# A fused decoder layer on one core: the expert biases move from the thirteenth pair of experts to the tenth, and the last pair gets another assignment of PSUM banks and another order on TensorE

## The reference, cut to what matters here

```python
def moe_ffn(hx, ...):                       # hx: 288 x 1024
    logits = hx @ w_router + b_router       # 32 experts
    top_val, top_idx = lax.top_k(logits, 4)
    comb = ...                              # 288 x 32: softmax of the four, 0 elsewhere
    def expert_step(acc, xs):               # for each of the 32 experts
        gu = hx @ wgu + bgu                 # 1024 -> 2048
        gate = jnp.minimum(gu[:, 0::2], 7.0)
        up = jnp.clip(gu[:, 1::2], -7.0, 7.0)
        act = gate * jax.nn.sigmoid(1.702 * gate) * (up + 1.0)
        y = act @ wdn + bdn                 # 1024 -> 1024
        return acc + c[:, None] * y
hx = layer_norm(DN_ALPHA * hx + moe_ffn(hx, ...), ln2_g, ln2_b)
```

## Time and profile before

| | |
|---|---|
| median of 3 runs | 1140.02 us (1139.33 to 1140.36) |
| the profiled execution | 1139.37 us, span 1137.5 us |
| TensorE busy | 1099.5 us, 97% of the span |
| VectorE, ScalarE busy | 293.1 us (26%), 203.6 us (18%) |
| DMA | 454.37 MB, mean 399 GB/s, over 420 GB/s in most slices after the first quarter |
| chain that ended last | PE 83%, DMA 13%, ACT 2%, DVE 2% |

### The profile page before, as it was taken

How to read it: one execution, slowest core, us unless ns; L and a number is a source line. 1 busy time by engine, 2 the same in 40 slices (tenths; PEclk the granted TensorE clock), 3 DMA queues, 4 the chain that set the end, 5 groups by cost and what they waited for, 6 DMA issues and landing times.

```text
span 1137.5 us, 14116 instructions
## 1 busy us (share of the span) xinstructions
PE 1099.5 (97%) x5468; PEld 463.2 (41%) x5469; DVE 293.1 (26%) x734; ACT 203.6 (18%) x481; POOL 30.0 (3%) x65
## 2 busy tenths in 40 slices
PE   8999999999999999999999999999999999999996
PEld 6876764433333333333333333333333333333331
DVE  1553757530303030212121212120203031303033
ACT  2323412411111120202020202020201111111102
POOL 0110111000000000000000000000000000000001
PEclk9999999999999999999999999999999999999998
DMA  9967878999999999999999999999999999999994
GB/s 361 351 219 248 285 280 336 426 433 407 430 421 430 430 431 430 431 430 429 432 431 432 432 430 432 432 432 429 433 430 432 432 430 432 431 430 430 425 426 160
DMA packets 59172, 454.37 MB, mean 399 GB/s; under 512 B 6467, under 2 KB 19411, under 8 KB 31348
## 3 DMA queue, kind: packets, MB, share of 16 engines
q1 hardware_dynamic: 56642, 440.97, 92.7%
q0 software_dynamic: 1728, 10.75, 2.5%
q10 hardware_dynamic: 754, 1.98, 0.4%
HBM read 450.14 MB, written 11.93 MB: 406 GB/s over the span
## 4 chain that ended last, share of the span: by engine, by line
PE 83%; DMA 13%; ACT 2%; DVE 2%; issue 1%; SPq 0%; DVEq 0%
PE bank L1171 30%; PE bank L1224 19%; DMA ring<-in_w_gate_up 13%; PE bank L732 6%; PE bank L759 6%; PE bank L1055 5%; PE bank L1251 3%; PE bank L762 2%; PE bank L920 2%; PE bank L1051 1%; PE bank L1354 1%; PE bank L1267 1%; PE bank L877 1%; ACT ybuf L1417 1%; ACT actT L1417 1%; PE bank L851 1%
## 5 line engine op out<-in xcount | busy, mean ns | idle before, releaser
L1171 PE MATMUL bank<-ring,xg 128*64 128x512 f32 x2032 | 445.6, 594 | 10.8 <-DMA ring<-in_w_gate_up 10.8
L1171 PEld LDWEIGHTS bank<-ring,xg 128*64 128x64 f32 x2032 | 146.4, 137 | 299.3 <-issue 296.9
L1224 PE MATMUL bank<-ring,actT 128*64 128x512 f32 x960 | 216.2, 597 | 4.2 <-ACT actT L1417 4.2
L2080 DVE TENSOR_TENSOR acc<-acc,bank 128x512 f32<-128x512 f32 x60 | 41.3, 688 | 492.0 <-PE bank L1251 491.8
L1571 ACT ACTIVATE sig<-gate 128x256 f32<-128x256 f32 x64 | 26.5, 416 | 530.1 <-DVE gate L2062 530.1
L1224 PEld LDWEIGHTS bank<-ring,actT 128*64 128x64 f32 x960 | 67.3, 137 | 120.0 <-issue 115.3
L2062 DVE TENSOR_SCALAR gate<-bank 128x256 f32<-128x256 f32 x64 | 26.8, 419 | 186.8 <-PE bank L1171 186.8
L759 PE MATMUL bank<-xT,wblk 128*128 128x288 f32 x256 | 65.4, 409 | 0.3 <-DVE xT L1670 0.3
L1562 ACT ACTIVATE xg<-bank,small 128x128 f32<-128x128 f32 x128 | 48.0, 457 | 97.0 <-PE bank L732 96.9
L1055 PE MATMUL bank<-hx,pick 128*128 128x512 f32 x128 | 59.2, 605 | 0.0
L1417 ACT ACTIVATE ybuf<-bank 128x512 f32<-128x512 f32 x63 | 36.0, 596 | 126.7 <-PE bank L1224 87.4
(11 more groups left out here) (247 smaller groups left out, 672.3 us busy)
## 6 DMA issues: line engine op xcount, KB each, us to landing
ring<-in_w_gate_up SPq DMA_DIRECT2D x127, 2048.0 KB, 26.5
ring<-in_w_down SPq DMA_DIRECT2D x63, 2048.0 KB, 28.0
wblk<-in_w_in SPq DMA_DIRECT2D x11, 1024.0 KB, 8.7
kring<-in_cache_k_moba SPq DMA_DIRECT2D x16, 256.0 KB, 7.5
vring<-in_cache_v_moba SPq DMA_DIRECT2D x16, 256.0 KB, 7.2
out<-in_state_k_win POOLq DMA_DIRECT2D x8, 512.0 KB, 5.2
out<-in_state_v_win POOLq DMA_DIRECT2D x8, 512.0 KB, 6.1
kring<-in_state_k_win SPq DMA_DIRECT2D x16, 256.0 KB, 5.3
```

Source lines behind the costliest of these rows:

```text
L1171: ins = nc.tensor.matmul(bank[n][64 * e:64 * e + 64, :], xg[:, k, 64 * e:64 * e + 64], w[e][:, 512 * n:512 * n + 512], start=False, stop=( ...
L1224: ins = nc.tensor.matmul(bank[4 + half][64 * e:64 * e + 64, :], actT[:, j, 64 * e:64 * e + 64], w[e][:, at:at + 512], start=(j == 0), stop ...
L2080: V.tensor_tensor(o, o, new, ALU.add).then_inc(S.added, 1)
```

## The change

Two parts. `MIDDLE` becomes 9: the biases are added in pair 9, and pairs 9 to 15 instead of 12 to 15 are written out on TensorE. In the last pair, `combine` of pair 14 follows gate/up step k = 1 instead of k = 3; tile 0 and the samples are brought into banks 4, 5 and 7 after k = 4, ahead of gate/up's end; both halves of the activations are transposed into bank 6, the first behind a wait for the copy of the weights out of that bank; down's sums go to banks 0 and 1; the rest follows the new assignment of banks.

```diff
+    Y_BANK, SUM_BANK = (0, 1), ((4, 5), (2, 3), (7,))
...
-    MIDDLE = 12
+    MIDDLE = 9
...
         finish(MIDDLE + 1, MIDDLE // PERIOD, 1, MIDDLE // PERIOD)
+        finish(MIDDLE + 2, MIDDLE // PERIOD, 2, MIDDLE // PERIOD + 1)
+        finish(MIDDLE + 3, MIDDLE // PERIOD + 1, 0, MIDDLE // PERIOD + 1)
+        finish(MIDDLE + 4, MIDDLE // PERIOD + 1, 1, MIDDLE // PERIOD + 1)
         last = PAIRS - 1
...
-            return nc.tensor.matmul(bank[2 * t + half][:, :], ident, acc[:, t, 512 * half:512 * half + 512],
+            return nc.tensor.matmul(bank[SUM_BANK[t][half]][:, :], ident, acc[:, t, 512 * half:512 * half + 512],
                                     start=True, stop=stop)
 
-        def last_down():
-
-            turn_act(last, 2 * last + 2, (0,))
+        def keep_first():
             pe.wait_ge(S.added, 5 * last + 5)
             keep_sums(0, 0)
             keep_sums(0, 1)
-            pe.wait_ge(S.actT_ready, last * 2 + 1)
             keep_sums(2, 0)
+
+        def turn_last(a):
+            pe.wait_ge(S.act_ready, last * 4 + 2 * a + 2)
+            pe.wait_ge(*((S.actT_ready, 2 * last + 1) if a else (S.spread_ready, last + 1)))
+            for j in range(4 * a, 4 * a + 4):
+                f = 512 * a
+                ins = turn(bank[6][:, 128 * (j % 4):128 * (j % 4) + 128], up[:, f + j % 4:f + 512:4])
+            ins.then_inc(S.act_turned, 1)
+
+        def last_down():
+
+            turn_last(0)
             for v in range(4):
...
-                            ins = nc.tensor.matmul(bank[4 + half][64 * e:64 * e + 64, :], actT[:, j, 64 * e:64 * e + 64],
+                            ins = nc.tensor.matmul(bank[Y_BANK[half]][64 * e:64 * e + 64, :], actT[:, j, 64 * e:64 * e + 64],
...
                 if v == 0:
-                    turn_act(last, 2 * last + 2, (1,))
+                    turn_last(1)
                     keep_sums(1, 0)
...
-        gate_up(last, last // PERIOD, 0, {3: lambda: combine(last - 1), 5: lambda: turn_weights(last, 2 * last + 1)})
+        gate_up(last, last // PERIOD, 0, {1: lambda: combine(last - 1), 4: keep_first, 5: lambda: turn_weights(last, 2 * last + 1)})
         last_down()
         mix_last()
...
-        take_turned(PAIRS - 1, (0,))
+        take_turned(PAIRS - 1, (0,), (6, 6))
         sigmoids(PAIRS - 1, (2, 3))
-        take_turned(PAIRS - 1, (1,))
+        take_turned(PAIRS - 1, (1,), (6, 6))
```

More of the change, by code:

```diff
@@ L1329, in keep_sums @@
             if t == 2:
-                return nc.tensor.matmul(bank[7][:, 0:256], ident, acc_s[:, :], start=True, stop=stop)
-            return nc.tensor.matmul(bank[2 * t + half][:, :], ident, acc[:, t, 512 * half:512 * half + 512],
+                return nc.tensor.matmul(bank[SUM_BANK[2][0]][:, 0:256], ident, acc_s[:, :], start=True, stop=stop)
+            return nc.tensor.matmul(bank[SUM_BANK[t][half]][:, :], ident, acc[:, t, 512 * half:512 * half + 512],
                                     start=True, stop=stop)
-        def last_down():
-            turn_act(last, 2 * last + 2, (0,))
+        def keep_first():
             pe.wait_ge(S.added, 5 * last + 5)
@@ L1370, in mix_last @@
                 if t == 2:
-                    ins = mix_samples(bank[7], False)
+                    ins = mix_samples(bank[SUM_BANK[2][0]], False)
                 else:
-                    ins = nc.tensor.matmul(bank[j][:, :], spread[:, 128 * t:128 * t + 128],
+                    ins = nc.tensor.matmul(bank[SUM_BANK[t][half]][:, :], spread[:, 128 * t:128 * t + 128],
                                            ybuf[:, 512 * half:512 * half + 512], start=False, stop=True)
                 ins.then_inc(S.mixed, 1)
-        gate_up(last, last // PERIOD, 0, {3: lambda: combine(last - 1), 5: lambda: turn_weights(last, 2 * last + 1)})
+        gate_up(last, last // PERIOD, 0, {1: lambda: combine(last - 1), 4: keep_first, 5: lambda: turn_weights(last, 2 * last + 1)})
         last_down()
@@ L1575, in take_weights, with take_turned @@
             copy(spread[:, :], bank[6][:, 0:T]).then_inc(S.spread_ready, 1)
-        def take_turned(i, halves=(0, 1)):
+        def take_turned(i, halves=(0, 1), banks=(7, 6)):
             for a in halves:
                 act.wait_ge(S.act_turned, i * 2 + (a + 1))
-                copy(actT[:, 4 * a:4 * a + 4, :], bank[7 - a][:, :].rearrange("p (k s) -> p k s", k=4)).then_inc(
+                copy(actT[:, 4 * a:4 * a + 4, :], bank[banks[a]][:, :].rearrange("p (k s) -> p k s", k=4)).then_inc(
                     S.actT_ready, 1)
@@ L1636, in take_lower @@
             act.wait_ge(S.down_done, PAIRS)
-            copy(ybuf[:, 0:512], bank[4][:, :]).then_inc(S.y_ready, 1)
+            copy(ybuf[:, 0:512], bank[Y_BANK[0]][:, :]).then_inc(S.y_ready, 1)
         nc.scalar.activation(s_(c_junk), s_(c_junk), ACT.Sqrt)
@@ L1649, in _ @@
         for half in range(2):
-            nc.scalar.activation(acc[:, 0, 512 * half:512 * half + 512], bank[half][:, :], ACT.Identity,
+            nc.scalar.activation(acc[:, 0, 512 * half:512 * half + 512], bank[SUM_BANK[0][half]][:, :], ACT.Identity,
                                  bias=mv[:, 2:3], scale=mv[:, 1:2]).then_inc(S.y_centred, 1)
@@ L2138, in take_upper @@
             dve.wait_ge(S.down_done, PAIRS)
-            V.tensor_copy(ybuf[:, 512:1024], bank[5][:, :]).then_inc(S.y_ready, 1)
+            V.tensor_copy(ybuf[:, 512:1024], bank[Y_BANK[1]][:, :]).then_inc(S.y_ready, 1)
         def sums_to_sbuf():
@@ L2144, in sums_to_sbuf @@
                 t, half = divmod(j, 2)
-                o, new = (acc[:, t, 512 * half:512 * half + 512], bank[j][:, :]) if t < 2 else (acc_s[:, :], bank[7][:, 0:256])
+                o, new = (acc[:, t, 512 * half:512 * half + 512], bank[SUM_BANK[t][half]][:, :]) if t < 2 else (acc_s[:, :], bank[SUM_BANK[2][0]][:, 0:256])
                 dve.wait_ge(S.mixed, 5 * last + n + 1)
@@ L2159, in y_statistics @@
                 dve.wait_ge(S.mixed, 5 * last + after + half)
-                step.on(V.bn_stats(s_(c_stat + 12 * t + 6 * half, 6), bank[2 * t + half][:, :]))
+                step.on(V.bn_stats(s_(c_stat + 12 * t + 6 * half, 6), bank[SUM_BANK[t][half]][:, :]))
             dve.wait_ge(step.sem, step.n)
@@ L2196, in _ @@
             c = slice(512 * half, 512 * half + 512)
-            gain_and_bias(acc[:, 1, c], bank[2 + half][:, :], mv[1][:, 0:1], mv[1][:, 1:2], ln2_g_sb[:, c], ln2_b_sb[:, c])
+            gain_and_bias(acc[:, 1, c], bank[SUM_BANK[1][half]][:, :], mv[1][:, 0:1], mv[1][:, 1:2], ln2_g_sb[:, c], ln2_b_sb[:, c])
     ctx.close()
```

## The result

| | before | changed |
|---|---|---|
| median (lowest to highest), 11 runs each | 1141.07 us (1139.33 to 1142.12) | 1144.03 us (1142.09 to 1144.80) |
| profiled execution, span | 1139.37, 1137.5 us | 1142.41, 1140.6 us |
| ratio | | 1.0021, 95% interval 1.0014 to 1.0029 |

The changed kernel is slower by some 2.4 us (1.6 to 3.3 by the interval; the medians lie 2.96 apart). Forecast were 0.9 us more and "within 0.2%"; the ratio lies at that bound. The median of 1144.03 us lies outside the forecast range of 1139.3 to 1142.3. A part of that distance, 1.05 us, is no effect of the change: the 11 runs of the kernel before have a median of 1141.07, where the forecast added its 0.9 to the 1140.02 of the three runs shown.

The account below looks back on a forecast made before the run. The prediction took the DMA queue's weights, 58.35 us a pair, to set the pace mid-kernel. Its terms, 0 + 0 + 0.9 + 0, added to the median 1140.02 us, gave 1140.9 us, range 1139.3 to 1142.3.

Parts of the forecast that it names:

- The biases' place is worth nothing: Biases moved from pair 12 to 9: TensorE's 4.8 us is caught up waiting for weights either way; 0 us.
- The waits of about 1 us in pairs 12 to 14: Sign of being right: TensorE waits about 1 us for weights in gate/up of these pairs.
- The rival by which they would be worth 4.8 us: TensorE bounds from pair 12 to the end, so moving the biases wins 4.8 us: 1136.1 us; chance 0.08.
- The loops that become straight code cost nothing that the rows show: Newly written-out pairs on TensorE: 0 us, since pair 14, already straight, takes 55.95 us.
- its signs of being wrong: Pair 15's bias rows near 1062, weight wait in last pair, down's clock under 1.00, DVE awaiting a DMA before statistics.
- nothing to lose, since the wait that remains is the queue's: Bound on the biases' move, at pair 14's step 6: at most 0.14 us to gain, no loss.
- The last pair: Gate/up's end to down: moved identity products and uncovered activation copy cost net +0.9 us, between +0.75 and +1.0.
- The identity products after k = 4: Tile 0 and the samples, moved into the last pair's gate/up, add 2.3 us there (2.15 to 2.35).
- the way from transposes to down: Last pair: transposes, then ACT's copy with nothing between, put down's start 1.53 us after the transposes start.
- the cover that is lost: Last pair: identity products no longer run during ACT's copy; the old 2.91 us to down is subtracted.
- LayerNorm rows: Last LayerNorm's gain and bias, issued 2.3 us later: cost 0, 1.1 us cover; rival, DVE waits, 1142.2 us, chance 0.05.
- clock: Rival: TensorE's clock falls in the joined gap before the last pair's down, +3.6 us, 1144.5 us; chance 0.04.

Follow-up runs that it names:

- the second time: The unmodified changed kernel run once more against the kernel before: median 1144.22 against 1141.80 us, ratio 1.0025 (1.0013 to 1.0036).

## Why the prediction was wrong

*The biases' place is worth nothing: right.* The waits of about 1 us in pairs 12 to 14 are there (1.72 at 922.94, 0.95 at 981.18 and 1039.52), TensorE runs at the pace of the weights in both kernels, and the biases in pair 2 bring nothing either. The rival by which they would be worth 4.8 us had read the chain alone.

*"The loops that become straight code cost nothing that the rows show": wrong,* and this is the step that failed. I had tested it on TensorE's own time for a written-out pair (55.95 us), where it costs nothing indeed. But I had just found that the DMA engines and not TensorE set the pace, and did not ask what the code does to those. The page of the kernel before lists 34 packets of instructions in queue q8, and the windows show none of them in the looped stretch up to 892 us and two in each written-out pair. The runs show what six more of them do: about 1.0 us in the mean of the traces (1.6 against 0.6 above), 1.4 in the profiled execution. The bias rows of pair 15 start at 1069.11, not at the 1067.1 that the forecast named; among its signs of being wrong it had only an earlier start. I also gave the term the wrong bound: "nothing to lose, since the wait that remains is the queue's" takes the queue's pace for fixed.

*The last pair: right in kind, undersized.* Forecast 0.9, measured 1.18. The identity products after k = 4 cost 1094.38 - 1092.04 = 2.34 (2.3 forecast), the way from transposes to down 1.52 (1.53). Two terms were off: I took the 2.91 of the chain for the cover that is lost, where the time line's own 2.84 answers to it, 0.07; and gate/up now runs in four blocks instead of three, of 7.01, 10.46, 3.59 and 7.09 us where it was 13.89, 7.02 and 7.09, so 0.15 more. By the end of down both are on the path.

*LayerNorm rows and clock: cost 0, as forecast.* DVE starts its statistics 1.2 us behind the start of TensorE's first product, as before, without a wait for the DMA issued at 1111.11. The forecast had the cover shrink from 2.5 to 1.1 us; it grew to 3.6, since the last issue moved by 2.1 us and not with gate/up's end, while DVE's start moved by 3.15. The granted clock in down is 1.00, and its steps keep 3.65 us.

**Together:** 1.2 from the last pair and 1.0 from the code make 2.2 us, against 2.4 measured (1.6 to 3.3) and 2.9 (1.5 to 4.1) the second time. What is left over is within the intervals and stays open. The single parts are too small to be told by whole times (ratios of 1.0003 each); they rest on the traces. Which engine a packet goes to, and whether that differs from run to run by a rule, stays open.

## What to carry to other kernels

Where a stretch is bound by DMA, everything that uses the DMA engines belongs into the account, the kernel's own instructions too: writing out a loop on a busy engine can slow a transfer that has nothing to do with it. Work that is moved ahead of a wait for data can be worth nothing, as the 4.8 us here, even where the chain of waits holds it; look for the next moment at which data binds again. And an independent product is worth most where TensorE would wait for a copy, as between the transposes and down here: count what idle time it fills before moving it, and split it when there are two such gaps.

## What was unexpected of the hardware

While weights fill the DMA engines, the first of the 16 increments keeps a pace that repeats to 0.02 us over 408 us. The last of them lags for good: by 0.9 to 1.9 us at step 7 of the first pair, by 2.6 to 6.9 at that of pair 14. From pair 7 on packets of instructions of 16 KB do it, one engine and 1.45 us at a time; for the time before that, when other transfers run too, what does it stays open. With fewer pairs written out, a loop of three pairs runs on TensorE from 590 to 1040 us without one such packet.
